# Plain fp32 matmuls in place of three-part fp32r products in all weight products of a four-block model

## The chip, the cores and the metric

The kernel runs on one core of one Trainium2 chip. The metric is the device time of one launch in microseconds (us), over three runs. Smaller is better.

## The reference

The model works on 512 latent tokens and 256 context tokens of width 1024, all in fp32. It has four blocks:

- the even layer: `x W_in`, from which come latent attention (its two lora products `mla_w_uq` 384 to 768 and `mla_w_ukv` 256 to 1024, 8 heads of 96) and a gated depthwise convolution; then `W_out`, added to x under a gate; then a mixture of 16 experts with expert choice;
- the odd layer: `x W_in` for windowed attention and for a recurrence with decay (WKV), `W_out`, and a second mixture;
- forgetting attention: `rmsnorm(x) W_in` (3 x 1024 + 16 columns), 16 heads, `W_out`, then a convolving feed-forward;
- sparse attention: `rmsnorm(x) W_kv` and `rmsnorm(x) W_in`, compressed, selected and window keys, `W_out`, and a second such feed-forward.

A convolving feed-forward is, for each of 22 tiles of 128 hidden channels:

```
up   = h @ w_up[:, tile]         # h = rmsnorm(x), 512 x 1024
gate = h @ w_gate[:, tile]
both: causal depthwise convolution of 3 taps along the tokens
x += (silu(conv(up)) * conv(gate)) @ w_down[tile, :]
```

## The kernel before

The program is a row of stages. Each has an instruction block for every engine (sync = SP, tensor = PE, vector = DVE, scalar = ACT, gpsimd = POOL) and ends with a barrier of all engines (L70 in the profile). Within a stage the order on each engine is written out by hand, and semaphores tie the engines together.

All products with weights, but for the mixtures', the modulation's (`ada_w`) and the recurrence's small loras, are computed in three parts. A number is split into a high part, which is its rounding to the type fp32r (float32r), and a low part, the rest: ACT writes the high part with a copy, DVE subtracts it for the low part. A product is then `hi*hi + hi*lo + lo*hi`, three fp32r matmuls that add up in PSUM. The contraction always runs in steps of 128 (k), so each output tile of a 1024-wide input takes 8 x 3 matmuls. The functions are these:

- `linear` (L493): weights come in pieces of 256 columns through a ring `w_landing`. `hi_part` (ACT) and `lo_part` (DVE) split each piece into `w_hi` and `w_lo`; PE waits for the semaphore `split`, and SP reloads a slot of the ring when it has been split. With `whole` the input rows, too, are split in this stage (L595, L615). It is called for the two lora products of the even layer, for the odd layer's recurrence inputs (15 tiles of 128 features, tokens in 512 + 256), and by `add_gated` for both layers' `W_out`.
- `normed_linear` (L640): normalises rows of x, transposes them on PE (L740), scales (and, with a shift, shifts) them into `h`, splits them, and multiplies. It is called for the inputs of the even layer, the odd layer's attention, forgetting attention (`haT`, `a_w_in`), the sparse keys (`hbT`) and the sparse queries (`hqT`).
- `product_norm` (L1003): `W_out` of the two last attentions, with the residual, the norm and the transposes for the feed-forward behind it.
- `conv_ffn` (L3362): 44 chunks of weights of 128 x 1024 for the products up and gate (L3437), then 22 for down (L3450), through a ring of 4 landing slots and 3 slots of high and low parts. ACT runs two chunks ahead (`AHEAD`). The hidden rows are split as well (L3478, L3493).
- `paired_attention` (L1406) writes the output of the two last attentions as a high and a low part (L1590, L1592).

The inner product of `conv_ffn`:

```
3434 for k in range(KD):
3436     for i, (w, h) in enumerate(((wh, hh), (wh, hl), (wl, hh))):
3437         mm = nc.tensor.matmul(ps[c % 4][:, :], w[:, c % NP, cols], h[:, k, :], ...)
```

Products that are plain fp32 already are those of the mixtures (L2044, L2056: `out[n*64:(n+1)*64] = v[:, k, 0:64]^T @ land[...512 columns]`, for 2 mixtures, 16 experts, 8 k and 2 halves n per weight matrix), the scores of latent attention (L1475 `kT,qT`, 96 rows; 8 heads: 32 products with 512 columns and 48 with 256), the recurrence's loras (L2896, 64 rows) and a product with the compressed values (L1498).

Of the kernel before, what the change touches and what calls it, by code (L numbers as in the profile page):

```python
# [14 lines left out]
P = 128  # L15
# [333 lines left out]
def norm_turn(nc, x, width, outT, segments, ident, keep=None, lowT=None, early=None, mod=None, chunks=(), first=False,  # L349
              taps=None):  # L350
# [10 lines left out]
    with Stage(nc) as st:  # L361
        junk = st.sb("squares", [P, width])
        xn = keep if keep is not None else st.sb("normed", [P, n, width])
# [12 lines left out]
        hi_ready = st.sem("hi_ready")  # L376
        low_ready = st.sem("low_ready")
        shifted = lowT is not None and segments[0][3] is not None
        part = st.sb("low_unshifted", [P, 4, 512]) if shifted else None
        units = [(first, count, gain, shift, k) for first, count, gain, shift in segments for k in range(K)]  # L380
        mod_ps = [st.ps(f"ada_ps{i}", [P, 512]) for i in range(4 if mod is not None else 0)]
        block = st.block()

        @block.sync
        def _(sp):
            if first:
                mod.load_first(sp)
            if early is not None:
                early.load_first(sp)
            if mod is not None:  # L390
                mod.sync(sp, chunks)
                mod.store(sp, chunks)

        @block.scalar
        def _(act):
            for i, t in enumerate(tiles):
                if i:

                    act.wait_ge(squared, i)
                nc.scalar.activation(junk[:, :], x[:, t, 0:width], ACT.Square, accum_out=ss[:, i:i + 1]) \  # L400
                    .then_inc(squared, 1)
            act.wait_ge(mean_ready, 1)
            nc.scalar.activation(rt[:, :], rms[:, :], ACT.Sqrt).then_inc(root_ready, 1)
            if mod is not None:
                mod.keep_partial(act, chunks[0], mod_ps)
            if lowT is not None:
                u = 0
                for first, count, gain, shift in segments:
                    for k in range(K):
                        act.wait_ge(turned, u + 1)  # L410
                        to, src = outT[:, k, first * P:(first + count) * P], ps[u % 4][:, 0:count * P]
                        if shift is None:
                            ins = nc.scalar.activation(to, src, ACT.Copy, scale=gain[:, k:k + 1])
                        else:
                            ins = nc.scalar.activation(to, src, ACT.Identity, scale=gain[:, k:k + 1],
                                                       bias=shift[:, k:k + 1])
                        ins.then_inc(hi_ready, 1)
                        u += 1
            if mod is not None:
                mod.keep_partial(act, chunks[1], mod_ps)  # L420
                mod.keep_total(act, chunks[0], mod_ps)
                mod.keep_total(act, chunks[1], mod_ps)

        @block.vector
        def _(dve):
            if taps is not None:
                taps.add(dve, 6)
# [8 lines left out]
            u = 0  # L436
            for first, count, gain, shift in segments:
                for k in range(K):
                    dve.wait_ge(turned, u + 1)
                    to = outT[:, k, first * P:(first + count) * P]  # L440
                    if lowT is not None:
                        dve.wait_ge(hi_ready, u + 1)
                        low = lowT[:, k, first * P:(first + count) * P]
                        if shifted:
                            if u >= 4:
                                dve.wait_ge(low_ready, u - 3)
                            low = part[:, u % 4, 0:count * P]
                        ins = nc.vector.scalar_tensor_tensor(
                            out=low, in0=ps[u % 4][:, 0:count * P],
                            scalar=gain[:, k:k + 1], in1=to.bitcast(F32), op0=ALU.mult, op1=ALU.subtract)  # L450
                    elif shift is None:
                        ins = nc.vector.tensor_scalar(to, ps[u % 4][:, 0:count * P], gain[:, k:k + 1], None, ALU.mult)
                    else:
                        ins = nc.vector.tensor_scalar(to, ps[u % 4][:, 0:count * P], gain[:, k:k + 1],
                                                      shift[:, k:k + 1], ALU.mult, ALU.add)
                    ins.then_inc(kept, 1)
                    u += 1
                    if taps is not None:
                        taps.add(dve, 2)
            if taps is not None:  # L460
                taps.add(dve, 10)
            if shifted:
                dve.wait_ge(low_ready, len(units))

        @block.gpsimd
        def _(pool):
            for u, (first, count, gain, shift, k) in enumerate(units if shifted else ()):
                pool.wait_ge(kept, u + 1)
                nc.gpsimd.tensor_scalar(lowT[:, k, first * P:(first + count) * P], part[:, u % 4, 0:count * P],
                                        shift[:, k:k + 1], None, ALU.add).then_inc(low_ready, 1)  # L470

        @block.tensor
        def _(pe):
            u = 0
            if mod is not None:
                mod.partial(pe, chunks[0], mod_ps)
            for first, count, gain, shift in segments:
# [9 lines left out]
            if mod is not None:  # L487
                mod.partial(pe, chunks[1], mod_ps)
                mod.total(pe, chunks[0], mod_ps)
                mod.total(pe, chunks[1], mod_ps)  # L490


def linear(nc, h, K, w, jobs, RING=3, whole=None, low_from=None, beside=(), mod=None, then=None, early=None, residual=None,  # L493
           taps=None, tap_every=1):
# [6 lines left out]
    hh, hl = h  # L501
# [3 lines left out]
    whole_tiles = sorted({t for job in jobs for t in job[3]}) if whole is not None else []  # L505
# [8 lines left out]
    with Stage(nc) as st:  # L514
        land = st.sb("w_landing", [P, RING, K, PW]) if early is None else early.land
        wh, wl = (st.sb(f"w_{n}", [P, RING, K, PW], F32R) for n in ("hi", "lo"))
        ps = [st.ps(f"lin_ps{i}", [P, 512]) for i in range(NB)]
        landed = [st.sem(f"w_landed{i}") for i in range(RING)] if early is None else early.landed
        low_landed = [st.sem(f"low_landed{k}") for k in range(K if low_from is not None else 0)]
        beside_done = st.sem("beside_done")  # L520
        hi_ready = st.sem("w_hi_ready")
        split = st.sem("w_split")
        rows_hi = st.sem("rows_hi_ready")
        rows_split = st.sem("rows_split")
# [6 lines left out]
        def _(sp):  # L531
            for c, (job, a, b) in enumerate(pieces):
                if early is not None and c < RING:
                    continue
                if c >= RING:
                    sp.wait_ge(split, c - RING + 1)
                sp.dma_start(land[:, c % RING, :, 0:b - a], wv[:, :, job[1] + a:job[1] + b]).then_inc(landed[c % RING], 16)
            if mod is not None:
                mod.load_first(sp)

        @block.gpsimd
        def _(pool):
            for k in range(len(low_landed)):
                pool.dma_start(hl[:, k, :], low_from[:, k, :]).then_inc(low_landed[k], 16)
# [6 lines left out]
        def _(pe):  # L551
            u = 0
            for c, piece in enumerate(pieces):
                job, a, b = piece
                pe.wait_ge(split, c + 1)
                for unit in units(piece):
                    if u >= NB:
                        pe.wait_ge(kept, u - NB + 1)
                    if job[0] == "tok":
                        t = unit[0]  # L560
                        if t in whole_tiles:
                            pe.wait_ge(rows_split, whole_tiles.index(t) + 1)
                        out = ps[u % NB][:, 0:b - a]
                        cols = slice(t * P, (t + 1) * P)
                    else:
                        f, (r0, r1) = unit
                        out = ps[u % NB][:, 0:r1 - r0]
                        cols = slice(r0, r1)
                        fs = slice(f * P - a, (f + 1) * P - a)
                    for j, (x, v) in enumerate(((hh, wh), (hh, wl), (hl, wh))):  # L570
                        for k in range(K):
                            if u == 0 and j == 2 and low_landed:
                                pe.wait_ge(low_landed[k], 16)
                            if job[0] == "tok":
                                lhsT, rhs = x[:, k, cols], v[:, c % RING, k, 0:b - a]
                            else:
                                lhsT, rhs = v[:, c % RING, k, fs], x[:, k, cols]
# [4 lines left out]
        @block.scalar  # L582
        def _(act):
            def hi_part(c):
                if c < len(pieces):
                    _, a, b = pieces[c]
                    act.wait_ge(landed[c % RING], 16 * (c // RING + 1))
                    if c >= RING:
                        act.wait_ge(summed, before[c - RING + 1])
# [7 lines left out]
            for c in range(1, len(pieces)):  # L597
                hi_part(c)
# [3555 lines left out]
```

## Time and profile before

| | us |
|---|---|
| runs, median of 3 | 4164.89 (4163.84 to 4169.29) |
| profiled execution, span | 4167.8 |
| PE busy (matmul) | 3632.9, 87% |
| PE weight loads busy | 2565.1, 62% |
| DVE busy | 1958.1, 47% |
| ACT busy | 1143.7, 27% |
| POOL busy | 648.3, 16% |
| mean DMA rate | 158 GB/s, 660.04 MB |

The profile covers one execution. The page gives no time for it but its span, which lies between the fastest and the slowest of the three runs and 2.9 us above their median; differences are worked out against the span. A record of PE is one matmul instruction as the hardware ran it; its duration contains the time through the array, so in a dense run the distance from one record's start to the next says what a matmul costs, not its duration. PEclk 1.00 stands for the full granted clock.

### The profile page before, as it was taken

Reading aid. Unit: us, or ns where it says so; the run is one execution under the profiler, and the core shown is the slowest. Engines: PE = TensorE matmul, PEld = TensorE weight load, DVE = VectorE, ACT = ScalarE, POOL = GpSimd, SP = SyncE. Lnnn points to the kernel's source line nnn. Section 1 sums busy time; section 2 is a strip of 40 time slices with the busy share of each in tenths; the row PEclk is TensorE's granted clock in tenths of the full one; section 3 lists DMA queues with packets and bytes.
Section 4 is the critical chain, followed back from the end, with each engine's and each line's share of the span. In section 5 each row is a group of like instructions: output and inputs, shape, how many; then the busy total and the mean of one; then the engine's idle time right before and its main releaser. Section 6 shows DMA issues by size and latency. Waiting matters only on the chain. (4 is left out here: it accounts for less than half of the span.)

```text
span 4167.8 us, 71056 instructions
## 1 busy us (share of the span) xinstructions
PE 3632.9 (87%) x29972; PEld 2565.1 (62%) x29972; DVE 1958.1 (47%) x3688; ACT 1143.7 (27%) x2375; POOL 648.3 (16%) x687
## 2 busy tenths in 40 slices
PE   5978878999979897989769777798899997899999
PEld 4845663444448783858553222396788776677877
DVE  4688751001045556756640000255477445656762
ACT  2124510000023413434310000225432223663221
POOL 0014400111102301525200000014100001430000
PEclk8998888999989998989889999999999998999999
DMA  4142248999941213010269999810123221012322
GB/s 171 58 162 63 77 185 315 394 395 394 394 146 80 89 49 115 4 43 4 95 233 401 402 401 400 309 56 21 63 91 96 91 93 43 22 47 66 96 91 81
DMA packets 195492, 660.04 MB, mean 158 GB/s; under 512 B 27708, under 2 KB 86076, under 8 KB 145368
## 3 DMA queue, kind: packets, MB, share of 16 engines
q1 hardware_dynamic: 182392, 621.16, 39.7%
q0 software_dynamic: 12784, 34.35, 3.2%
q8 instruction: 238, 3.90, 0.4%
q14 instruction: 78, 0.64, 0.0%
HBM read 626.01 MB, written 29.44 MB: 157 GB/s over the span
## 5 line engine op out<-in xcount | busy, mean ns | idle before, releaser
L3488 DVE TENSOR_TENSOR ffn_w_lo<-ffn_landing,ffn_w_hi 128x1024 fp32r<-128x1024 f32 x128 | 156.9, 1226 | 295.7 <-ACT ffn_w_hi L3466 295.7
L3437 PE MATMUL ffn_ps<-ffn_inT_hi,ffn_w_hi 128*128 128x512 f32 x704 | 279.2, 397 | 3.5 <-PEq L70 3.5
L3437 PE MATMUL ffn_ps<-ffn_inT_lo,ffn_w_hi 128*128 128x512 f32 x704 | 278.1, 395 | 0.0
L3437 PE MATMUL ffn_ps<-ffn_inT_hi,ffn_w_lo 128*128 128x512 f32 x704 | 277.4, 394 | 0.0
L2044 PE MATMUL up_ps<-w_quarter,rowsT 128*64 128x512 f32 x1024 | 235.9, 602 | 38.5 <-DMA w_quarter<-in_moe_w 38.4
L2044 PE MATMUL down_ps<-w_quarter,hiddenT 128*64 128x512 f32 x1024 | 236.4, 601 | 32.3 <-DMA w_quarter<-in_moe_w 30.3
L2044 PE MATMUL gate_ps<-w_quarter,rowsT 128*64 128x512 f32 x1024 | 236.6, 608 | 27.6 <-DMA w_quarter<-in_moe_w 18.8
L1960 POOL DMA_INDIRECT summed_dram<-gains_then_rows,part_row x48 | 74.7, 1557 | 932.1 <-DVE gains_then_rows L2174 927.2
L2104 ACT ACTIVATE rowsT<-misc_ps 128x384 f32<-128x384 f32 (+1 forms) x64 | 27.9, 438 | 603.9 <-PE misc_ps L2033 602.3
L2167 DVE TENSOR_TENSOR gain_then_hidden<-up_ps,gain_then_hidden 128x768 f32<-128x768 f32 (+1 forms) x32 | 26.4, 825 | 352.2 <-PE up_ps L2056 181.3
L2044 PEld LDWEIGHTS down_ps<-w_quarter,hiddenT 128*64 128x64 f32 x1024 | 68.6, 136 | 190.5 <-issue 129.9
L3466 ACT ACTIVATE ffn_w_hi<-ffn_landing 128x1024 fp32r<-128x1024 f32 x128 | 134.9, 1054 | 183.3 <-PE ffn_ps L3450 165.5
L2044 PEld LDWEIGHTS up_ps<-w_quarter,rowsT 128*64 128x64 f32 x1024 | 67.8, 137 | 184.0 <-issue 109.3
L2044 PEld LDWEIGHTS gate_ps<-w_quarter,rowsT 128*64 128x64 f32 x1024 | 69.6, 139 | 174.8 <-issue 119.9
L2174 DVE SCALAR_TENSOR_TENSOR gains_then_rows<-down_ps,part_gates,row_gain 128x512 f32<-128x512 f32 (+1 forms) x48 | 30.3, 659 | 311.9 <-PE down_ps L2056 170.4
L1530 ACT ACTIVATE probT<-probT_ps 128x384 f32<-128x384 f32 (+3 forms) x336 | 145.9, 455 | 96.9 <-PE probT_ps L1485 95.4
L2160 DVE COPY hiddenT<-misc_ps 128x512 f32<-128x512 f32 (+1 forms) x48 | 27.4, 599 | 306.1 <-PE misc_ps L2074 306.1
L3437 PEld LDWEIGHTS ffn_ps<-ffn_inT_hi,ffn_w_hi 128*128 128x128 f32 x704 | 133.5, 190 | 34.5 <-issue 4.2
L3437 PEld LDWEIGHTS ffn_ps<-ffn_inT_hi,ffn_w_lo 128*128 128x128 f32 x704 | 133.4, 190 | 31.0
L3437 PEld LDWEIGHTS ffn_ps<-ffn_inT_lo,ffn_w_hi 128*128 128x128 f32 x704 | 133.6, 190 | 29.3
L1567 DVE TENSOR_REDUCE negmax<-score_ps 128x1 f32<-128x128 f32 (+4 forms) x240 | 131.0, 546 | 27.8 <-PE score_ps L1475 26.2
L2112 ACT ACTIVATE gain_then_hidden<-gate_ps 128x768 f32<-128x768 f32 (+1 forms) x32 | 22.6, 705 | 380.2 <-PE misc_ps L2074 360.0
(727 smaller groups left out, 8348.0 us busy)
## 6 DMA issues: line engine op xcount, KB each, us to landing
w_quarter<-in_moe_w SPq DMA_DIRECT2D x384, 1024.0 KB, 18.1
ffn_landing<-in_f_w_up SPq DMA_DIRECT2D x88, 512.0 KB, 3.5
ada_ring<-in_ada_w SPq DMA_DIRECT2D x80, 512.0 KB, 5.4
ffn_landing<-in_f_w_down SPq DMA_DIRECT2D x44, 512.0 KB, 3.5
w_landing<-in_od_w_in SPq DMA_DIRECT2D x13, 1024.0 KB, 6.1
w_landing<-in_a_w_in SPq DMA_DIRECT2D x12, 1024.0 KB, 5.0
ada_landing<-in_ada_w SPq DMA_DIRECT2D x8, 1024.0 KB, 12.5
w_landing<-in_ev_w_in SPq DMA_DIRECT2D x6, 1024.0 KB, 5.7
```

What stands on the lines that cost most here:

```text
L1530: nc.scalar.activation(pT[:, i % ST, a:b], pt[k % 2][:, 0:b - a], ACT.Copy).then_inc(tkept, 1)
L1567: nc.vector.reduce_max(mx[:, m:m + 1], score(i, 0, n), AX_X, negate=True).then_inc(maxed, 1)
L1960: nc.gpsimd.indirect_dma_start(out=to, out_offset=bass.IndirectOffsetOnAxis(ap=pidx[:, part, e:e + 1], axis=0), in_=ys[e % 2][:, cols], in ...
L2044: mm = nc.tensor.matmul(out[n * 64:(n + 1) * 64, 0:LW], v[:, k, 0:LR], land[c][:, kk, n * LW:(n + 1) * LW], start=(k == 0), stop=(k == KD ...
L2104: nc.scalar.activation(xs[:, half * HK:(half + 1) * HK, :], misc[half][:, 0:HK * R].rearrange("p (k r) -> p k r", k=HK), ACT.Copy).then_in ...
L2112: nc.scalar.activation(hid[:, 0:W], p1[:, 0:W], ACT.Silu).then_inc(silu_ready, 1)
L2160: nc.vector.tensor_copy(hT[:, :, r0:r0 + r].rearrange("p (n j) r -> p j n r", n=n), misc[part][:, 0:KD * r].rearrange("p (j n r) -> p j n ...
L2167: tt(hid[:, 0:W], p3[:, 0:W], hid[:, 0:W], ALU.mult).then_inc(hid_ready, 1)
L2174: last = nc.vector.scalar_tensor_tensor(out=ys[e % 2][:, cols], in0=py[:, cols], scalar=gall[:, part, e:e + 1], in1=g2r[:, cols], op0=ALU. ...
L3437: mm = nc.tensor.matmul(ps[c % 4][:, :], w[:, c % NP, cols], h[:, k, :], start=(k + i == 0), stop=(k == KD - 1 and i == 2))
L3466: nc.scalar.activation(wh[:, c % NP, :], land[:, c % NL, :], ACT.Copy).then_inc(hi_ready, 1)
L3488: nc.vector.tensor_tensor(wl[:, c % NP, :], land[:, c % NL, :], wh[:, c % NP, :].bitcast(F32), ALU.subtract).then_inc(split, 1)
```

## The change

Each of the products named above becomes one plain fp32 matmul per k, with the weights as they landed and the rows as they are. With this go: the high and low buffers, the copies on ACT and the subtractions on DVE that filled them, the semaphores `split`, `w_hi_ready`, `rows_split`, and the odd layer's low rows, which were stored to DRAM and fetched again (3.1 MB each way, POOL's queue). PE waits for the landing itself; SP reloads a slot when its products are summed. The rings grow where space became free: 6 pieces (5 in the even layer, 3 for the sparse keys; before 3 or 2) in `normed_linear`, 6 (before 2) for the recurrence inputs, 7 chunks (before 4) in `conv_ffn`, and all four pieces of `W_out` in `product_norm`. The transposed rows of `normed_linear` and `product_norm` are now written half by ACT and half by DVE (`left_half`, `right_half`). In `norm_turn` ACT writes them alone. The feed-forward's DVE multiplies straight into `hidden`; its helper work for the sparse positions (`side`) stands behind the last convolution. The attentions write one output.

```diff
 def linear(...)
-                    sp.wait_ge(split, c - RING + 1)
+                    sp.wait_ge(summed, before[c - RING + 1])
...
-                pe.wait_ge(split, c + 1)
+                pe.wait_ge(landed[c % RING], 16 * (c // RING + 1))
...
-                    for j, (x, v) in enumerate(((hh, wh), (hh, wl), (hl, wh))):
-                        for k in range(K):
...
-                            mm = nc.tensor.matmul(out, lhsT, rhs, start=(j + k == 0), stop=(j == 2 and k == K - 1))
+                    for k in range(K):
+                        if job[0] == "tok":
+                            t = unit[0]
+                            mm = nc.tensor.matmul(ps[u % NB][:, 0:b - a], h[:, k, t * P:(t + 1) * P],
+                                                  land[:, c % RING, k, 0:b - a], start=(k == 0), stop=(k == K - 1))
...
-            hi_part(0)
-            for t in whole_tiles:
-                nc.scalar.activation(hh[:, :, t * P:(t + 1) * P], whole[:, :, t * P:(t + 1) * P], ACT.Copy) \
-                    .then_inc(rows_hi, 1)
-            for c in range(1, len(pieces)):
-                hi_part(c)
...
 def conv_ffn(...)
-    NL, NP, UP = 4, 3, 2 * F_TILES
+    NL, UP = 7, 2 * F_TILES
...
             for c in range(NL, CHUNKS):
-                if c >= NL + AHEAD:
-                    sp.wait_ge(split, c - NL + 1 - AHEAD)
-                sp.dma_start(land[:, c % NL, :], source(c)).then_inc(landed[c % NL], 16)
+                sp.wait_ge(used, c - NL + 1)
+                ffn.load(sp, c)
...
                 for k in range(KD):
-                    cols = slice(k * P, (k + 1) * P)
-                    for i, (w, h) in enumerate(((wh, hh), (wh, hl), (wl, hh))):
-                        mm = nc.tensor.matmul(ps[c % 4][:, :], w[:, c % NP, cols], h[:, k, :],
-                                              start=(k + i == 0), stop=(k == KD - 1 and i == 2))
+                    mm = nc.tensor.matmul(ps[c % 4][:, :], land[:, c % NL, k * P:(k + 1) * P], hT[:, k, :],
+                                          start=(k == 0), stop=(k == KD - 1))
```

Two places show what each engine issues. On PE, the start of the product with `a_w_in` in `normed_linear` (stage 33: `turn_ps` takes the transposes, `lin_ps` the sums, `haT` are the rows). Before:

```order
L740 MATMUL turn_ps_33<-ident,normed 128x128 x24
L771 MATMUL lin_ps_33<-w_hi,haT 128x256 x8
L771 MATMUL lin_ps_33<-w_lo,haT 128x256 x8
L771 MATMUL lin_ps_33<-w_hi,haT 128x256 x8
L740 MATMUL turn_ps_33<-ident,normed 128x128 x8
```

Now:

```order
L619 MATMUL turn_ps_33<-ident,normed 128x128 x24
L639 MATMUL lin_ps_33<-w_landing,haT 128x256 x8
L619 MATMUL turn_ps_33<-ident,normed 128x128 x8
L639 MATMUL lin_ps_33<-w_landing,haT 128x256 x376
L644 MATMUL lin_ps_33<-haT,w_landing 16x512 x8
```

The order stays; 24 matmuls of a unit become 8. On DVE, two chunks of the second feed-forward (`conv_1` takes the convolutions). Before:

```order
L3488 TENSOR_TENSOR ffn_w_lo<-ffn_landing,ffn_w_hi 128x1024
L3504 TENSOR_SCALAR conv_1<-ffn_ps_48,f_conv_w,f_conv_b 128x512
L3505 SCALAR_TENSOR_TENSOR conv_1<-ffn_ps_48,f_conv_w,conv_1 128x511
L3507 SCALAR_TENSOR_TENSOR conv_1<-ffn_ps_48,f_conv_w,conv_1 128x510
L3493 TENSOR_TENSOR hidden_lo<-conv_1,hidden_hi 128x512
```

Now:

```order
L3230 TENSOR_SCALAR conv_1<-ffn_ps_48,f_conv_w,f_conv_b 128x512
L3231 SCALAR_TENSOR_TENSOR conv_1<-ffn_ps_48,f_conv_w,conv_1 128x511
L3233 SCALAR_TENSOR_TENSOR conv_1<-ffn_ps_48,f_conv_w,conv_1 128x510
L3239 TENSOR_TENSOR hidden<-conv_1 128x512
L3230 TENSOR_SCALAR conv_1<-ffn_ps_48,f_conv_w,f_conv_b 128x512
```

The two subtractions are gone and the convolutions follow each other directly.

## Rows read from the trace of the kernel before

**Rows 1.** The page: PE's busy time, granted clock in 40 slices.

```profile
PE 3632.9 (87%) x29972; PEld 2565.1 (62%) x29972; DVE 1958.1 (47%) x3688; ACT 1143.7 (27%) x2375; POOL 648.3 (16%) x687
...
PEclk8998888999989998989889999999999998999999
```

**Rows 2.** Stretches with the changed products; one of thirteen, then their sum.

```profile
core 0: us, PE busy (x) PEld busy (x) DVE busy (x) ACT busy (x) POOL busy (x), PEclk, DMA share, GB/s
...
3014.10:3386.90 372.80, 372.22 (x1584) 299.12 (x1584) 211.11 (x259) 94.10 (x111) 0.00 (x0) 0.99 0.28 88
...
sum 1620.30, PE 1587.07 PEld 1393.88 DVE 909.52 ACT 365.07 POOL 40.72; mean PE 122.08 PEld 107.22 DVE 69.96 ACT 28.08 POOL 3.13
```

**Rows 3.** Stretches, PE and PEld of L3437, L3450, L771, L578 alone.

```profile
3040.00:3240.00 200.00, 200.00 (x859) 160.80 (x858) 1.00 0.30 93
...
3280.00:3370.00 90.00, 90.00 (x389) 72.75 (x388) 1.00 0.26 80
...
2700.00:2820.00 120.00, 120.00 (x1025) 120.00 (x1024) 1.00 0.23 72
...
520.00:570.00 50.00, 50.00 (x419) 50.00 (x418) 1.00 0.00 1
```

**Rows 4.** Groups on PE: busy, mean ns, idle before, releaser.

```profile
L2044 PE MATMUL up_ps<-w_quarter,rowsT 128*64 128x512 f32 x1024 | 235.9, 602 | 38.5 <-DMA w_quarter<-in_moe_w 38.4
...
L1475 PE MATMUL score_ps<-kT,qT 96*128 96x512 f32 x64 | 37.0, 662 | 2.3 <-PEq L70 1.7 <-ACT ada_ring L1539 0.7
...
L1498 PE MATMUL out_ps<-cmp_probsT,v_cmp 128*128 128x128 f32 x64 | 12.6, 280 | 0.0
```

**Rows 5.** Timeline of PE in the first mixture: start, length, engine, line.

```profile
1052.18 7.09 PE L2044 MATMUL up_ps<-w_quarter,rowsT 128*64 128x512 f32 x32
1059.20 3.66 PE L2056 MATMUL up_ps<-w_quarter,rowsT 128*32 128x256 f32 x64
1062.79 7.09 PE L2044 MATMUL down_ps<-w_quarter,hiddenT 128*64 128x512 f32 x32
```

**Rows 6.** Timeline of PE's weight loads: latent scores, a recurrence lora.

```profile
458.24 0.19 PEld L1475 LDWEIGHTS score_ps<-kT,qT 96*128 96x128 f32 x1 [0.24 <-issue]
458.67 0.19 PEld L1475 LDWEIGHTS score_ps<-kT,qT 96*128 96x128 f32 x1 [0.24 <-issue]
...
1841.02 0.62 PEld L2896 LDWEIGHTS lora_ps<-lora_in,x 64*128 64x128 f32 x3 [0.24 <-issue]
1841.88 0.19 PEld L2896 LDWEIGHTS lora_ps<-lora_in,x 64*128 64x128 f32 x1 [0.24 <-issue]
```

**Rows 7.** Waits of PE: line, releaser, total us, times, longest.

```profile
PE lin_ps L578 <- DVE mixedT_lo L615: 28.3, 2, 20.9
PE lin_ps L578 <- DVE w_lo L608: 17.3, 3, 11.1
PE lin_ps L771 <- DVE h1T_low_1a L879: 13.3, 4, 7.2
PE lin_ps L771 <- DVE h1T_low L879: 12.0, 4, 6.1
PE lin_ps L771 <- DVE w_lo L873: 7.2, 3, 2.8
...
PE out_ps L1045 <- DVE fa_w_lo L1158: 2.9, 1, 2.9
```

**Rows 8.** Timeline of ACT at the start of the recurrence inputs' stage.

```profile
1420.59 1.91 ACT L590 ACTIVATE w_hi<-w_landing 128x2048 fp32r<-128x2048 f32 x1 [8.50 <-DMA w_landing<-in_od_w_in]
```

**Rows 9.** Waits, 2868 to 2954, same columns.

```profile
PEld out_ps L1504 <- DVE fa_out_lo L1592: 2.7, 9, 1.0
```

**Rows 10.** The page: the splitting's largest group, and two kinds of loads.

```profile
L3488 DVE TENSOR_TENSOR ffn_w_lo<-ffn_landing,ffn_w_hi 128x1024 fp32r<-128x1024 f32 x128 | 156.9, 1226 | 295.7 <-ACT ffn_w_hi L3466 295.7
...
ffn_landing<-in_f_w_up SPq DMA_DIRECT2D x88, 512.0 KB, 3.5
...
w_landing<-in_od_w_in SPq DMA_DIRECT2D x13, 1024.0 KB, 6.1
```

More of the change, by code:

```diff
@@ L362, in norm_turn @@
         junk = st.sb("squares", [P, width])
-        xn = keep if keep is not None else st.sb("normed", [P, n, width])
+        xn = st.sb("normed", [P, n, width])
         ss = st.sb("sum_squares", [P, n])
@@ L375, in norm_turn @@
         kept = st.sem("kept")
[L376 to L381, printed above, removed]
+        mod_ps = [st.ps(f"ada_ps{i}", [P, 512]) for i in range(4)]
         block = st.block()
@@ L387, in _ @@
                 mod.load_first(sp)
[L388 to L392, printed above, removed]
+            early.load_first(sp)
+            mod.sync(sp, chunks)
+            mod.store(sp, chunks)
         @block.scalar
@@ L403, in _ @@
             nc.scalar.activation(rt[:, :], rms[:, :], ACT.Sqrt).then_inc(root_ready, 1)
[L404 to L408, printed above, removed]
-                    for k in range(K):
[L410 to L422, printed above, removed]
+            mod.keep_partial(act, chunks[0], mod_ps)
+            u = 0
+            for first, count, gain in segments:
+                for k in range(K):
+                    act.wait_ge(turned, u + 1)
+                    nc.scalar.activation(outT[:, k, first * P:(first + count) * P], ps[u % 4][:, 0:count * P], ACT.Copy,
+                                         scale=gain[:, k:k + 1]).then_inc(kept, 1)
+                    u += 1
+            mod.keep_partial(act, chunks[1], mod_ps)
+            mod.keep_total(act, chunks[0], mod_ps)
+            mod.keep_total(act, chunks[1], mod_ps)
         @block.vector
         def _(dve):
-            if taps is not None:
-                taps.add(dve, 6)
+            taps.add(dve, 6)
             dve.wait_ge(squared, n)
@@ L435, in _ @@
                     .then_inc(normed, 1)
[L436 to L470, printed above, removed]
+            taps.add(dve, 10 + 4 * K)
         @block.tensor
@@ L474, in _ @@
             u = 0
-            if mod is not None:
-                mod.partial(pe, chunks[0], mod_ps)
-            for first, count, gain, shift in segments:
+            mod.partial(pe, chunks[0], mod_ps)
+            for first, count, gain in segments:
                 pe.wait_ge(normed, first - t0 + count)
@@ L486, in _, with linear @@
                     u += 1
[L487 to L501, printed above, removed]
+            mod.partial(pe, chunks[1], mod_ps)
+            mod.total(pe, chunks[0], mod_ps)
+            mod.total(pe, chunks[1], mod_ps)
+def linear(nc, h, K, w, jobs, RING=3, beside=(), then=None, early=None, residual=None, taps=None, tap_every=1):
     PW, NB = 256, 8
@@ L669, in normed_linear @@
         xn = st.sb("normed", [P, 2, D])
-        shifted = any(shift is not None for _, shift in column.values())
-        part = st.sb("shifted", [P, 2, HK, P]) if shifted else None
         ss, rs, eps = st.sb("sum_squares", [P, nt]), st.sb("inverse_root", [P, nt]), st.sb("eps", [P, 1])
@@ L736, in turn_tile @@
                     if i >= 2:
-                        pe.wait_ge(rows_split if not shifted else moved, 2 * (i - 2) + half + 1)
+                        pe.wait_ge((left_rows, right_rows)[half], i - 1)
                     for k in range(HK):
@@ new lines, in right_half @@
+                dve.wait_ge(turned, 2 * i + 2)
+                for k in range(HK, KD):
+                    to, src = h[:, k, t * P:(t + 1) * P], tp[i % 2 * 2 + 1][:, k - HK, :]
+                    if shift is None:
+                        ins = nc.vector.tensor_scalar(to, src, gain[:, k:k + 1], None, ALU.mult)
+                    else:
+                        ins = nc.vector.tensor_scalar(to, src, gain[:, k:k + 1], shift[:, k:k + 1], ALU.mult, ALU.add)
+                ins.then_inc(right_rows, 1)
@@ L1000, in _, with product_norm @@
                 dve.wait_ge(head_gained, len(order))
-def product_norm(nc, parts, w, x, early, bufs, gain, nT, ffn, side):
-    (oh, ol), (hh, hl) = parts, nT
-    wh, wl, xn, row = bufs
-    HK, NL, NC = KD // 2, 2, 4
+def product_norm(nc, o, w, x, early, bufs, gain, hT, ffn, side):
+    more, xn, row = bufs
+    HK, NC = KD // 2, 4
     wv = w.rearrange("(g k p) n -> g p k n", p=P, k=HK)
@@ L3205, in odd_layer @@
+        rg = [(0, SEQ), (SEQ, TOK)]
+        linear(nc, hT, KD, d["od_w_in"],
+               [("feat", 0, 512, rg, shifted(U, 0, 0)), ("feat", 512, 512, rg, shifted(U, 4, 4)),
+                ("feat", 1024, 512, rg, shifted(VF, 0, 8)), ("feat", 1536, 384, rg, shifted(T, 0, 12))], RING=6,
+               beside=odd_loads)
         kk, LW = hT[:, 0:4, :], hT[:, 4:8, :]
@@ L3532, in _ @@
                 ins.then_inc(row_added, 1)
+        for c in range(NL):
+            loaded[NL * layer + c] += len(range(c, CHUNKS, NL))
 TWO_PI = 2 * np.pi
```

605 lines of the change are left out of this document (192 added, 413 removed).

## The prediction

> **What bounds the kernel now.** I read the page first: PE is busy for 87% of the span, and its clock is near full nearly throughout [rows 1]. A busy PE is not yet PE at its peak, so the second view is the stretches that hold the changed products, thirteen of them from the even layer's input at 62.4 us to the end of the second feed-forward at 4163.1. They last 1620.3 us, and PE is busy for 1587.1 of them, DVE for 909.5 and ACT for 365.1; in the first feed-forward PE is busy for 372.2 of 372.8 us [rows 2]. In these 1620 us, 39% of the span, TensorE sets the pace, and a change in its time per product goes into the total one to one, except where PE waits. The sum is made against the span of 4167.8 us; the median of the runs, 4164.9, lies 2.9 below it, and I subtract that at the end. About 0.2% (8 us) is what a measurement of this kernel can tell from no change.
>
> **What a three-part product costs.** Start to start, not duration, is the price in a dense run. 859 records of L3437 in 200 us are 0.233 us each; 389 of L3450 in 90 us are 0.231; 1025 of L771 with 256 columns in 120 us are 0.117; 419 of L578 in 50 us are 0.119 [rows 3]. Three such matmuls make a product: 0.699 us and 0.694 us with 512 columns, 0.351 and 0.358 with 256.
>
> **What a plain fp32 product costs.** Two things have to be seen. First, the hardware runs each as two records: the program has 512 products per weight matrix in L2044 and the trace 1024 records; 32 score products with 512 columns give 64; 32 openings with the compressed values give 64 [rows 4]. Second, a record takes twice as long per column as an fp32r one. In the mixture 32 records, which run two abreast in two halves of the array, take from 1052.18 to 1059.20, so 16 steps of 0.439; with 256 columns and four abreast, 64 records from 1059.20 to 1062.79 are 16 steps of 0.224 [rows 5]. Those steps contain the joins between runs. Without joins and not abreast: two weight loads of the scores stand 0.43 apart, and in the lora a load at 1841.02 is followed by three records (512, 256 and 256 columns) until 1841.88, 0.86 us, which gives 0.43 and 0.215 [rows 6]. These weight loads have 128 columns as the changed products have, take 0.19 us and are hidden under the record before. So a product costs 2 x 0.43 = 0.86 us with 512 columns and 0.43 with 256. I take this pair because it comes from a full-width stationary operand; the steps of the mixture (0.878 and 0.448) are kept as the upper end. Below 0.86 I see nothing.
>
> **The sum on TensorE.** Products changed, counted in the program: 704 up and gate, 352 down, and 344 others with 512 columns (128 in `W_out` of the last two attentions, 120 recurrence inputs, 64 in the even layer, 32 narrow ones); 384 with `haT` and 1150 others with 256 columns; 48 with 160.
> - 704 x (0.860 - 0.699) = +113; 352 x (0.860 - 0.694) = +58; 344 x 0.166 = +57.
> - 384 x (0.430 - 0.351) = +30; 1150 x (0.430 - 0.358) = +83.
> - 48 with 160 columns: two records of 160/256 x 0.215 = 0.134 against three that are held up by the weight load at about 0.11, so -3.
> Together +339 us, of which 171 in the two feed-forwards. At the head of each stage the clock is at its lower level for some microseconds after PE's wait; both forms lose half of that time, so I cost it at nothing.
>
> **What it takes away on the path.** PE waits for the splitting at the head of each stage. These waits add up to 83.4 us: 28.3 before `W_out` of the first two layers; 17.3 for split weights in `linear` (11.1 for the recurrence inputs, the rest for the two loras); 13.3 and 12.0 in `normed_linear` of the odd and the even layer; 7.2 in its other three calls; 2.9 before `W_out` of forgetting attention [rows 7], and 2.4 in a row like it for the sparse one. Not all of it goes; something else is late next:
> - `W_out` of the first two layers: the input rows are finished late anyway, and what goes is one copy of weights, one of rows and two subtractions, about 5.5 each: -11.
> - The two shifted `normed_linear` (13.3 and 12.0): rows went through four steps on DVE and ACT; now two halves in parallel. PE next waits for its own transposes and for the first piece: -12 and -10.5.
> - Recurrence inputs (11.1): ACT waited 8.50 us for the landing before its copy [rows 8]; the landing stays, copy 1.9 and subtraction 2.3 go: -4.3.
> - The loras -3; the three other calls' 7.2 and the earlier transposes of those stages -7.4 in all; the heads of `product_norm` -2.6 and its tails, where each half of the rows is now written once, -2.
> - The attentions write one output; PE waited 2.7 us for the second one in the first of them [rows 9]: -4 for both.
> Together -57. Bounds: all of the 83.4 and 12 us besides, -95; or only the copies and subtractions of one piece per stage, -30.
>
> **What costs or gives nothing.** The feed-forwards' subtractions (156.9 us in all) [rows 10] and ACT's copies before them lie under PE, which has under 1 us without work in the first feed-forward [rows 2]; their going frees engines that are not waited for. If they were the cover's other side, it would be DVE: it is busy for 211 of 372.8 us and only loses work. SP now reloads a slot when its products are done and not when it is split. That is later by up to a ring, but a landing takes 3.5 us against 8 x 0.86 = 6.9 us per chunk with six chunks ahead, and 6.1 us against at least 4 x 8 x 0.43 = 13.8 us per piece of 1 MB with two to five ahead [rows 10]; behind that wait stand only the next loads, and at the end of the last stage the stores, which come after the last load anyway. The low rows' 3.1 MB to DRAM and back ran beside work on POOL's queue: nothing. `side` moves behind the last convolution, under 150 us of PE.
>
> Net: 339 - 57 = +282; 4167.8 + 282 = 4450, less 2.9: **4447 us**. The forecast's own ends: 4165 + 339 - 95 = 4409 and, with the mixture's steps (2934 products x 0.018 = +53) and only 30 taken away, 4527.
>
> **The rivals.**
> - *One record's time per product: faster.* If the two records were a habit of products that fill only part of the array, or shorter ones in a full 128 x 128 product, a product would cost 0.43 and 0.215. TensorE's terms become 704 x -0.269, 352 x -0.264, 344 x -0.264, 384 x -0.136, 1150 x -0.143 and -9: -599; with -57, 3509 us. It decides once products cost 15% less than I take (282 of 1400 x 0.86 + 1534 x 0.43 = 1864 us), so 0.73 us with 512 columns. For it speaks only that no row has a full product of 512 or 256 columns; against it that 96-row, 64-row and 128-row ones all have two records [rows 4]. Chance 0.02. The Trainium skill (Perfetto Trace Analysis, Engine Utilization) gives TensorE's output rate for FP32_LOW_HIGH as half the full one, and read as a whole product's rate that is this rival. The trace shows half the rate for each record and two records, a quarter for the product; the rows decide against it.
> - *Plain records carry the excess that fp32r has: slower than forecast.* An fp32r record takes 0.231 to 0.233, while half a plain one is 0.215. If the 0.017 belongs to a weight load of 128 rows and 128 columns beside a stream of 128 rows, each of 5868 plain records has it too: +100, 4547 us. For: the plain loads of 128 columns have 96 and 64 rows [rows 6]. Against: the mixture's have 128 rows, and without joins they come to no more than 0.43. Chance 0.09.
> - *The later release of slots starves PE.* It decides where a landing outlasts the work ahead, 41 us in a feed-forward; loads would have to take ten times as long. If each of the 62 late chunks of both feed-forwards waited 3.5 us, +217: 4664. Chance 0.02.
> - *The products aren't what is waited for.* The total would move within 8 us. The stretches leave 33 us without PE in 1620, so no room. Chance 0.01.
>
> **How the numbers follow.** The forecast has 0.86, and 4447 us is its value. For 8 in 10 I take 4410 to 4505: it holds nearly all of the forecast's own spread but the corner where both bounds meet, and leaves out the rivals. Slower: 0.86 + 0.09 + 0.02 = 0.97; same 0.01; faster 0.02.
>
> **What would show it.** Right: PE's records in the changed products go from three to two each; a run of them in the feed-forward stands at 0.43; each feed-forward lasts about 459 us (372.8 + 86), PE's run on `haT` (384 products) about 165 us at 0.43 each; the idle time before `W_out` of the first two layers is near 17 us; DVE and ACT lose some 400 us of work and the end doesn't see it. Wrong: a record of 512 columns at 0.22 or at 0.45; waits of PE for `w_landing` or `ffn_landing` inside a stage; a granted clock below full in the middle of a feed-forward; or mixtures that last longer or shorter than before, which this sum takes to be untouched.

## The result and the profile after

The changed kernel took 4407.26, 4411.99 and 4416.46 us; the kernel before, beside it, 4162.27 to 4169.29. A fourth run of the changed kernel was disturbed (8169 us) and is left out. The ratio is 1.0585, 95% interval 1.0565 to 1.0605: slower by about 244 us, which makes 4408 us of the kernel before's 4164.4. The forecast was 4447 us with a range of 4410 to 4505: the direction was right, and the time lies 39 us below the forecast and 2 us below the range's low end. The 2 us are less than the measurement resolves (the interval spans 4400 to 4416 us, and the three runs by themselves have 4412 as their median); the 39 are not. The profiled execution has a span of 4405.3 us against 4167.8, +237.5 where the sum had +282. What follows looks for the missing 45 us.

The page of the changed kernel, answering [rows 1]:

```profile
PE 3948.6 (90%) x26990; PEld 2321.2 (53%) x26990; DVE 1570.7 (36%) x3229; ACT 851.2 (19%) x2086; POOL 641.5 (15%) x678
...
PEclk8989979999999989999899999999999998999999
```

PE is busy for 316 us more with 2982 fewer records. DVE and ACT lost 387 and 293 us of work.

Start to start in dense runs of the changed kernel, answering [rows 3] (columns: length, PE busy and records, granted clock, DMA share, GB/s): up and gate products of both feed-forwards, down products, `haT` with 256 columns.

```profile
core 0: us, PE busy (x), PEclk, DMA share, GB/s
3120.00:3320.00 200.00, 200.00 (x468) 1.00 0.24 76
4000.00:4200.00 200.00, 200.00 (x467) 1.00 0.26 76
3400.00:3520.00 120.00, 120.00 (x281) 1.00 0.19 57
2760.00:2880.00 120.00, 120.00 (x557) 1.00 0.12 36
```

200/468, 200/467 and 120/281 are 0.427 to 0.428 us per record, 120/557 is 0.215, two records per product. Taken were 0.43 and 0.215. The price was right, and with it two rivals fall: one record's time per product (0.22) and the excess of fp32r (0.447).

Stages from the last matmul of the stage ahead to their own last; only the border between `product_norm` and its feed-forward is put at the first matmul of the feed-forward. Before: even and odd `normed_linear`, WKV stretch, `product_norm`, the feed-forwards.

```profile
50.20:193.70 143.50, 130.34 (x864) 0.94 0.14 43
1188.00:1320.50 132.50, 103.14 (x816) 0.88 0.33 115
...
1552.40:2054.40 502.00, 431.81 (x9321) 0.92 0.15 52
...
2954.50:3014.10 59.60, 50.78 (x226) 0.94 0.23 82
3014.10:3386.90 372.80, 372.22 (x1584) 0.99 0.28 88
3789.30:4163.10 373.80, 367.91 (x1584) 0.98 0.28 90
```

The same stages after:

```profile
50.10:194.70 144.60, 144.60 (x592) 0.98 0.13 43
1195.50:1329.40 133.90, 118.28 (x561) 0.94 0.27 90
...
1586.00:2084.10 498.10, 431.70 (x9320) 0.93 0.15 53
...
3014.70:3078.60 63.90, 58.87 (x161) 1.00 0.27 101
3078.60:3533.70 455.10, 455.10 (x1056) 1.00 0.23 68
3945.50:4400.80 455.30, 455.22 (x1056) 1.00 0.24 71
```

Three things stand in these rows. The even layer's `normed_linear` has no time without PE any more (143.50 - 130.34 = 13.2 before). The granted clock rose in every one of these stages. And the two feed-forwards grew by 82.3 and 81.5 us, not 86.

Overlaying PE's records with the stretches in which the clock is at its lower level (1.2 instead of 2.4 GHz) gives the whole difference in three parts: time without PE, PE's work at the lower clock (half of it is time lost), and the rest, which is the products' price. Here every border is a last matmul, so the feed-forwards come to +162.6 and not to 82.3 + 81.5.

| stages (us, after minus before) | length | without PE | work at the lower clock | rest | waits as forecast |
|---|---|---|---|---|---|
| even and odd `normed_linear` | +2.5 | -26.9 | -15.3 | +37.1 | -22.5 |
| loras of the even layer | +0.4 | -6.5 | +1.8 | +6.0 | -3 |
| `W_out` of both layers | +13.1 | -11.0 | +1.6 | +23.3 | -11 |
| recurrence inputs | +25.2 | -4.9 | +0.5 | +29.8 | -4.3 |
| `haT`, `hbT`, compression, `hqT` | +28.7 | -11.5 | -18.3 | +49.3 | -7.4 |
| both `product_norm` | +11.1 | -6.4 | -8.8 | +22.0 | -4.6 |
| both feed-forwards | +162.6 | -7.6 | -10.5 | +175.5 | 0 |
| even attention and convolution | -3.5 | +2.4 | -12.9 | +0.6 | 0 |
| WKV | -3.9 | -3.8 | -1.2 | +0.5 | 0 |
| all others | +1.3 | -2.0 | +12.6 | -3.0 | -4 |
| sum | +237.5 | -78.2 | -50.6 | +341.0 | -57 |

So the products cost +341 (forecast +339), the time without PE fell by 78 (forecast 57), and the clock gave 50.6 / 2 = 25 (forecast 0). The stages that lost waits (`normed_linear`, `product_norm`, the feed-forwards) have 53 us less work at the lower clock. Where a wait only became shorter (the loras, `W_out`, the recurrence inputs) it stayed as it was, +4. The even attention's -12.9 and the others' +12.6, where no wait was removed, cancel. PE's waits after, answering [rows 7]:

```profile
PE lin_ps L495 <- PEq L69: 20.1, 4, 15.4
...
PE lin_ps L499 <- DMA w_landing<-in_od_w_in: 6.2, 1, 6.2
...
PE out_ps L870 <- DVE ffn_inT L940: 5.5, 2, 2.7
...
PE lin_ps L639 <- DMA w_landing<-in_od_w_in: 0.4, 1, 0.4
```

All of [rows 7] and its like, 83.4 us, are gone. In their place stand 20.1 (stage boundary before `W_out`, once 15.4), 6.2 (the first landing of the recurrence inputs) and 0.4: -57 net, the forecast's number. It is not the forecast's list, though. The forecast's -57 also held -2 for `product_norm`'s tails, part of -7.4 for transposes, and -4 for the attentions, and those -4 never came: the two attentions have 19.0 and 26.9 us without PE before, 18.6 and 27.4 after. The other 21 us are partly those transposes and tails and partly waits that the sum didn't list. One row of the kernel before shows the largest of these, a wait in the second feed-forward between the up and the down products:

```profile
PE ffn_ps L3450 <- DVE conv L3507: 6.5, 2, 5.9
```

The rest is in small ones: transposes that waited for split rows, `product_norm`'s (8.4 to 5.5), stage boundaries (the recurrence's loras waited 11.9, now 8.5).

### The profile page after: what moved, and what is told of

The parts are those of the page before. It is cut to its first block and busy times, and to the rows that moved or that the text cites. A ratio compares the mean times of both kernels' runs of the same rounds, so it can differ in the third digit from the quotient of the medians.

```text
span 4405.3 us, 64136 instructions
## 1 busy us (share of the span) xinstructions
PE 3948.6 (90%) x26990; PEld 2321.2 (53%) x26990; DVE 1570.7 (36%) x3229; ACT 851.2 (19%) x2086; POOL 641.5 (15%) x678
## 5 line engine op out<-in xcount | busy, mean ns | idle before, releaser
L3191 PE MATMUL ffn_ps<-ffn_inT,ffn_landing 128*128 128x512 f32 x1408 | 608.2, 595 | 2.2 <-PEq L69 2.2
L3191 PEld LDWEIGHTS ffn_ps<-ffn_inT,ffn_landing 128*128 128x128 f32 x1408 | 268.6, 191 | 340.8 <-issue 340.8
L3203 PE MATMUL ffn_ps<-ffn_landing,hidden 128*128 128x512 f32 x704 | 302.5, 592 | 0.0
L3203 PEld LDWEIGHTS ffn_ps<-ffn_landing,hidden 128*128 128x128 f32 x704 | 133.8, 190 | 168.4 <-issue 168.4
L3230 DVE TENSOR_SCALAR conv<-ffn_ps,f_conv_w,f_conv_b 128x512 f32<-128x512 f32 x88 | 71.2, 810 | 371.0 <-PE ffn_ps L3191 371.0
L639 PE MATMUL lin_ps<-w_landing,h1T 128*128 128x256 f32 (+1 forms) x800 | 166.6, 370 | 0.4 <-DMA w_landing<-in_od_w_in 0.4
L639 PE MATMUL lin_ps<-w_landing,haT 128*128 128x256 f32 x768 | 166.1, 379 | 0.0
L499 PE MATMUL lin_ps<-h1T,w_landing 128*128 128x512 f32 (+1 forms) x480 | 157.6, 492 | 6.2 <-DMA w_landing<-in_od_w_in 6.2
L639 PEld LDWEIGHTS lin_ps<-w_landing,haT 128*128 128x128 f32 x768 | 145.8, 190 | 19.7
L639 PEld LDWEIGHTS lin_ps<-w_landing,h1T 128*128 128x128 f32 x800 | 146.3, 190 | 18.4 <-DMA w_landing<-in_od_w_in 0.6
```

What stands on the lines that cost most here:

```text
L499: mm = nc.tensor.matmul(ps[u % NB][:, 0:r1 - r0], land[:, c % RING, k, f * P - a:(f + 1) * P - a], h[:, k, r0:r1], start=(k == 0), stop=(k ...
L639: mm = nc.tensor.matmul(ps[u % NB][:, 0:b - a], h[:, k, t * P:(t + 1) * P], land[:, c % RING, k, 0:b - a], start=(k == 0), stop=(k == KD - 1))
L3191: mm = nc.tensor.matmul(ps[c % 4][:, :], land[:, c % NL, k * P:(k + 1) * P], hT[:, k, :], start=(k == 0), stop=(k == KD - 1))
L3203: mm = nc.tensor.matmul(ps[2 * t + n][:, :], hidden[:, j, t * P:(t + 1) * P], land[:, c % NL, n * 512:(n + 1) * 512], start=(j == 0), stop ...
L3230: chain(nc.vector.tensor_scalar(to, src[:, :], fw[:, f, 2:3], fb[:, f:f + 1], ALU.mult, ALU.add))
```

## The experiments

Theory 1: the prices are right; the sum left out waits, and it left out the clock that a wait costs. Theory 2: the waits were sized right and a plain product is cheaper than 0.86. The first four kernels ran on one chip beside the kernel before (4166.17 us).

**Products alone.** In all five inner products of the kernel before, for example in `conv_ffn`:

```diff
-                    for i, (w, h) in enumerate(((wh, hh), (wh, hl), (wl, hh))):
-                        mm = nc.tensor.matmul(ps[c % 4][:, :], w[:, c % NP, cols], h[:, k, :],
-                                              start=(k + i == 0), stop=(k == KD - 1 and i == 2))
+                    mm = nc.tensor.matmul(ps[c % 4][:, :], wh.bitcast(F32)[:, c % NP, cols], hh.bitcast(F32)[:, k, :],
+                                          start=(k == 0), stop=(k == KD - 1))
```

> The kernel before, in which each three-part product is replaced by one plain fp32 matmul per k of the high parts; the low parts are still made and waited for but not used, so the low parts are left out of the result. All waits, copies and subtractions stay. Theory 1 (the sum's prices were right, and what the new structure takes away was sized too small): the products cost the forecast's +339 on their own, so 4500 to 4512 us. Theory 2 (plain products are cheaper than taken, the rest is as forecast): the measured +243 plus the forecast's 57 for waits, so about 4465 us.

Measured: 4486.57 us, ratio 1.0760 (1.0734 to 1.0787), +320. Between the two theories. The trace settles it: the rest is +351, so a product isn't cheaper. But the longer products cover waits by themselves: against the kernel before, time without PE falls by 18.4 and the work at the lower clock by 17.8. Its waits:

```profile
PE lin_ps L579 <- DVE mixedT_lo L616: 28.3, 2, 20.9
...
PE lin_ps L772 <- DVE h1T_low_1a L880: 9.5, 2, 6.4
PE lin_ps L772 <- DVE h1T_low L880: 9.4, 3, 6.1
```

The wait before `W_out` is untouched, those inside `normed_linear` shrank from 13.3 and 12.0, and the 6.5 us at L3507 are gone: DVE's convolutions, at an unchanged pace, are no longer behind PE. I had treated the price and the waits as two separate terms; they aren't.

**Structure alone.** A function `cut` shortens all matmuls but the first of each product (opening and up product shown):

```diff
+def cut(n, k, K):
+    share = {512: 0.8147, 256: 0.8295}.get(n, 1.0)
+    return n if k == 0 else round(n * (share * K - 1) / (K - 1))
...
-                    mm = nc.tensor.matmul(ps[c % 4][:, :], land[:, c % NL, k * P:(k + 1) * P], hT[:, k, :],
+                    n = cut(512, k, KD)
+                    mm = nc.tensor.matmul(ps[c % 4][:, 0:n], land[:, c % NL, k * P:(k + 1) * P], hT[:, k, 0:n],
```

> The changed kernel, in which all but the first matmul of each product run on fewer columns (for 512 columns: 402 of them with 8 k, 413 in the down products; for 256 columns: 206), so that a product takes what three fp32r matmuls took (0.699 and 0.358 us); the columns left out are left out of the result. It is the new structure at the old price. Theory 1: PE's idle time falls by 78 us and the time at the lower clock gives another 25, so 4165 - 103 = 4062 us, 4053 to 4072. Theory 2: 4165 - 57 = 4108 us.

Measured: 4092.91 us, ratio 0.9817 (0.9792 to 0.9841), -73. That is nearer to theory 2's number than to theory 1's, and 31 us off the latter. Time without PE fell by 73, near theory 1's 78. Two things ate most of the difference. The columns were cut to the price of the first feed-forward, which the second doesn't have (below): +8.1 there. And the WKV stretch, whose work doesn't change, ran 8 us longer, at a lower clock (0.90; 0.92 in the kernel before, in its row above):

```profile
1501.10:2011.10 510.00, 443.76 (x9321) 0.90 0.15 51
```

PE did 26.8 us more of its work at the lower clock there, which costs 13. So the clock in stages with sparse matmuls differs from kernel to kernel by as much as the effect sought, with unchanged work; why is not shown. In the changed stages the clock is that of the changed kernel: in the even and odd `normed_linear` PE does 9.6 us of its work at the lower clock (8.7 in the changed kernel, 24.0 before), in the two feed-forwards 6.4 (7.0 and 17.5). There the gain goes with the new structure and not with the products' price. With +320 and -73 the two halves add up to +247, against +244 for the whole change. That sum by itself doesn't decide, since each theory's own two halves add up to about as much; what excludes theory 2's cheap product is the records' spacing, 0.428 us, and the rest of +351. Both of theory 1's terms are there, in smaller size than I gave them.

**The clock by itself.** The kernel before, with matmuls in its waits:

```diff
+def keep_busy(nc, bank, n):
+    ident = BUSY["ident"]
+    for _ in range(n):
+        nc.tensor.matmul(bank[:, :].rearrange("p (k n) -> p k n", k=4), ident, ident.unsqueeze(1).broadcast_to([P, 4, P]),
+                         start=True, stop=True)
...
+                if c == 0:
+                    keep_busy(nc, ps[NB - 1], 7 if shifted else 3 if len(pieces) > 8 else 2)
                 pe.wait_ge(split, c + 1)
```

> The kernel before with matmuls of the identity on PE, 0.86 us each at the full clock, into a PSUM bank that is free, placed in the waits that the change removes inside normed_linear (7 at the first wait of the two shifted calls, 1, 1 and 3 at the later ones, 2 or 3 in the other calls) and in product_norm (2 at its head, 4 before its last transposes). No wait is shortened. If the missing time is partly the clock (in these stages the clock was low during about 40 us of PE's work, some 20 more than in the changed kernel): 10 to 20 us faster than before, 4145 to 4155 us. If the clock has no part in it: 4165 us, or a few us more where the added matmuls end late.

Measured: 4156.29 us over 10 runs, ratio 0.9967 (0.9952 to 0.9982): 10 us faster by doing more, the low edge of what was expected. In the kernel before, the clock over a wait in the odd `normed_linear`, the 5 us of products behind it, and then:

```profile
1209.10:1216.30 7.20, 0.05 (x1) 0.64 0.84 255
1216.30:1221.30 5.00, 4.99 (x23) 0.50 0.51 178
1221.30:1229.90 8.60, 8.60 (x75) 1.00 0.01 2
```

PE did nothing for 7.2 us, the clock fell during that time, and the first 5 us of products ran at half of it: 23 records where the next 8.6 us hold 75. With the wait filled, the stretch 2953.0 to 3008.6 (`product_norm`) and the head of the feed-forward:

```profile
2953.00:3008.60 55.60, 53.36 (x236) 1.00 0.25 88
3008.60:3382.20 373.60, 371.08 (x1585) 1.00 0.27 88
```

The clock in `product_norm` went from 0.94 to 1.00, and by the same two marks the stage went from 57.8 to 55.6 us. The stages with added matmuls got 16 us shorter together; all others together got 4 longer, WKV alone 3.8, again at a lower clock (0.91). The kernel's own work at the lower clock went from 264 to 238 us.

**Smaller rings.** `NL` 7 to 4 in `conv_ffn`, `RING` to 3 and 2 in `normed_linear` and `linear`, buffers in place.

```diff
-    NL, UP = 7, 2 * F_TILES
+    NL, UP = 4, 2 * F_TILES
```

> The changed kernel with rings as small as before: 4 chunks instead of 7 in the feed-forwards, 3 pieces instead of 6 or 5 in normed_linear, 2 instead of 6 for the recurrence inputs. If loads are hidden as forecast (3.6 us against 3 x 6.9 of work): 4408 us, within 4. If the larger rings are where the missing 40 us came from: about 4450 us, with waits of PE for the landings inside the stages.

Measured: 4411.87 us, ratio 1.0588 (1.0560 to 1.0615), the changed kernel's own. No wait of PE for `w_landing` or `ffn_landing` was added (6.2 and 0.4 us, as in the changed kernel), so the late slots starve nothing, with small rings or large.

**The waits put back.** The changed kernel, with a wait made by POOL (`waits_back`), and with that wait filled (`waits_back_busy`):

```diff
+            pool.wait_ge(turned, 6)
+            for i in range(16):
+                if i:
+                    pool.wait_ge(spent, i)
+                nc.gpsimd.memset(scratch[:, :], 0.0).then_inc(spent, 1)
...
+            pe.wait_ge(spent, 16)
             for c, piece in enumerate(pieces):
```

> The changed kernel, in which POOL clears a small scratch buffer 16 times in a row after the first three rows of tiles are transposed in each of the five normed_linear calls (about 6 us by POOL's other rows), and PE waits for it before the first product: a wait as the splitting made, and nothing else. If a wait costs only its own length: 5 x 6 to 7, so 30 to 35 us above the changed kernel's 4408, about 4441 us. If the clock it loses counts too, as I read the traces (3 to 5 us of it per wait): 45 to 60 us above, about 4460 us.

> waits_back with 7 matmuls of the identity on PE inside each of the five waits. If the clock is what a wait costs beyond its length, most of that comes back: 10 to 20 us faster than waits_back, about 30 to 38 us above the changed kernel. If not: the same as waits_back or a little slower.

Measured beside a kernel before of 4168.3 us: 4459.86, ratio 1.0698 (1.0671 to 1.0725), and 4450.74, ratio 1.0676 (1.0647 to 1.0705). The changed kernel's 1.0585 would be 4412 us on this chip, so the waits cost about 48 us and the page's wait row says how long they were:

```profile
PE lin_ps L646 <- POOL scratch L597: 33.0, 5, 6.9
```

In the trace the five stages (two of them with the mixture ahead) grew by 45.6 us for these 33.0, 1.4 us for each us of wait. PE did about 25 us more of its work there at the lower clock, and half of that, 12 us, is nearly all that came on top. In the odd layer, without the added matmuls:

```profile
1226.80:1233.70 6.90, 0.00 (x0) 0.62 1.10 347
1233.70:1238.70 5.00, 4.98 (x12) 0.50 1.10 349
1238.70:1245.00 6.30, 6.30 (x39) 1.00 0.58 192
```

and with them:

```profile
1228.70:1235.10 6.40, 6.38 (x18) 1.00 1.10 349
1236.00:1241.00 5.00, 4.99 (x27) 1.00 1.10 348
```

12 records in 5 us became 27. Eight of the 27 are transposes, which are shorter; like for like, the first 16 records of the product took 6.15 us without the added matmuls and 3.72 with them. Over the kernel this gave back 9 us (the intervals of the two overlap; the spans differ by 11.4), just short of the 10 to 20 expected. The added matmuls took 31 us and the time without PE fell by only 25: some of them ended late.

**Versions that beat both.** Added matmuls at the heads of stages and in the mixtures' selection too; and that with the first two tiles of `W_out` as plain products:

```diff
+                    if whole is not None and u < PLAIN:
+                        t = unit[0]
+                        for k in range(K):
+                            mm = nc.tensor.matmul(ps[u][:, 0:b - a], whole[:, k, t * P:(t + 1) * P], land[:, 0, k, 0:b - a],
+                                                  start=(k == 0), stop=(k == K - 1))
+                        mm.then_inc(summed, 1)
```

> The kernel before with the added identity matmuls of busy_inside and more of them where PE waits at the heads of stages (9 for the recurrence inputs, 3 before each W_out, 2 for the loras, 1 to 4 in normed_linear) and in the mixtures' selection of tokens (26 and 5 in the first, 19 and 8 in the second). No wait is shortened. If the clock follows PE's activity: the time at the lower clock while PE works falls by some 10 to 20 us more than with busy_inside, so 4145 to 4153 us. If busy_inside's 10 us were chance: 4165 us.

> busy_everywhere (without the 3 added matmuls before W_out), and in W_out of the first two layers the first two output tiles are plain fp32 products of the landed weights and the unsplit rows, all others three-part: PE needn't wait for the splitting there. The trace of the changed kernel has 5.5 us less idle time before each W_out; two plain tiles cost 2 x 8 x 0.074 = 1.2 us each and cover 6.9 us of splitting. If the waits went because nothing is split before the first product: 8 us faster than busy_everywhere, 4137 to 4146 us. If rows that are split late only move the wait behind the second tile: within 3 us of busy_everywhere.

Measured beside 4166.74 us: 4151.01, ratio 0.9959 (0.9945 to 0.9974), and 4147.47, ratio 0.9955 (0.9938 to 0.9972). Both are faster than the kernel before; the second isn't measurably faster than the first (its runs go from 4138 to 4160), and it missed the 4137 to 4146 expected. In `busy_everywhere` the kernel's own work at the lower clock fell by 58 us, worth 29; but the added matmuls took 137 us where the time without PE fell by 122, so 15 us of them were in the way. The second one's two `W_out` stages went from 78.6 and 68.4 us to 75.3 and 65.1, of which 3.4 us against `busy_everywhere` and not 8, since the filled waits had already won 3.2 there.

## Why the prediction was right, and where it failed

- *The price of a plain product* held: two records, 0.427 and 0.215 us at the full clock. The choice of the scores' and the lora's weight loads [rows 6] over the mixture's steps [rows 5] was the right one. The product takes 0.856 us, about four times its 512 columns at 2.4 GHz; the half rate that the Trainium skill gives for FP32_LOW_HIGH (Perfetto Trace Analysis, Engine Utilization) doesn't hold for a whole product.
- *The price of a three-part product* was read in the first feed-forward alone [rows 3], and the second is quicker. Records of L3437 in 190 us of each, before (the down products of L3450 stand alike in both, 389 in 90 us):

```profile
3060.00:3250.00 190.00, 190.00 (x816) 1.00 0.30 95
3835.00:4025.00 190.00, 190.00 (x840) 1.00 0.30 95
```

  0.2328 and 0.2262 us: 352 products x 3 x 0.0066 = 7 us more on the bill than the sum had. A plain record at 0.428 instead of 0.43 takes 1400 x 0.004 = 6 us off. The term came out at +341 for +339, partly by these two cancelling.
- *The step that failed*: "At the head of each stage the clock is at its lower level for some microseconds after PE's wait; both forms lose half of that time, so I cost it at nothing." Both forms lose it only where both wait. The change removes waits inside `normed_linear`, `product_norm` and the second feed-forward, and with them falls of the clock. The trace gives 25 us for this. The experiments show that it exists and its order: 10 us from filling some of the waits, about 15 us beyond the length of five waits that were put back. They don't confirm the 25 to the microsecond; the drift of the clock in WKV and other sparse stages is of the same size. The Trainium skill (TensorE: Matmul & The Clock Gate, HAM oscillation) describes this loss behind waits, paid again at each of them; the five waits put back agree, with 1.4 us per us of wait.
- *The second one*: "Together -57." Those waits gave 57, but time without PE fell by 78. I listed waits for the splitting and missed those caused by engines that the splitting kept busy. In particular "their going frees engines that are not waited for" was wrong for the second feed-forward, where PE waited 5.9 us for a convolution that stood behind subtractions on DVE. This row was in the view that I quoted from [rows 7]. The wait is gone in the products-alone kernel as well, where the subtractions stay, and in the structure-alone kernel, where the products are as quick as before: a slower PE or a freer DVE, either is enough. And the -4 for the attentions' single output was wrong: nothing came of it. That 57 was met to the microsecond is luck.
- *The lower bound* of 4409 took -95 for waits alone. Measured are -78 for waits and -25 for the clock, 103 together; the bound came so near because its surplus of 17 us for waits stood in for most of a clock term that it didn't have.
- *Costed at nothing, and right*: later release of slots, the low rows in DRAM, the move of `side`. Both mixtures lasted as before, within 1 us. The rival of late slots was dead, but its price was summed wrongly: 62 waits of 3.5 us are one feed-forward's, not both.
- *What was to be seen*: each feed-forward at 459 us (455.1 and 455.3: in the first, records of 0.428 instead of 0.43 take 2 us off, the wait and the clock at the head the rest); `haT`'s run near 165 (166.1 us busy); DVE and ACT down by some 400 (387 and 293, so 680 together); idle time before `W_out` of the first two layers near 17 (1.9 + 15.4).

## What to carry to other kernels

A wait on TensorE costs more than its length where the granted clock falls during it: here 1.4 us per us for waits of 6 to 7 us. When a change removes or adds a wait, look at the granted clock in the 5 us behind it, and bill the difference. When PE gets slower per product, the engines beside it get relatively faster, and waits for them shrink without being touched: price and waits are one sum. And read the price of the old form in each stage that uses it, not in one.

## What was not expected of the hardware

- The same fp32r matmul, in the same loop with the same operands' shapes, stood at 0.2328 us in one feed-forward and at 0.2262 in the other, while plain fp32 records stood at 0.427 and 0.428. The two differ in where the low weights lie in SBUF, and in the helper work `side` that runs beside the first one. Whether either is the cause is open; it wasn't tried.
- PE can be made faster by giving it more to do: the kernel before gained 0.4% from matmuls whose results nobody reads.
- A stretch whose work is the same in all kernels (WKV, 9320 records) took from 492.6 us (with the smaller rings) to 510.0 (structure alone), with a granted clock of 0.94 and 0.90; for kernels of the same structure, all that differs is what ran ahead of it. Differences below about 10 us in one profiled execution say nothing here without a look at the clock. The row with the smaller rings:

```profile
1588.50:2081.10 492.60, 426.15 (x9321) 0.94 0.15 53
```
